# The compression's chunks turned by VectorE in 32x32 blocks instead of by TensorE

## What is computed

```python
def compress(rows, pe, w1, w2):
    B, Tk = rows.shape[:2]
    n_chunk = Tk // CMP_STRIDE
    r = CMP_BLOCK // CMP_STRIDE
    n_cmp = n_chunk - r + 1
    chunks = rows[:, :n_chunk * CMP_STRIDE].reshape(B, n_chunk, CMP_STRIDE, N_KV_HEADS, HEAD_DIM)
    blocks = jnp.concatenate([chunks[:, j:j + n_cmp] for j in range(r)], axis=2) + pe[:, None, :]
    flat = blocks.transpose(0, 1, 3, 2, 4).reshape(B, n_cmp, N_KV_HEADS, CMP_BLOCK * HEAD_DIM)
    return jax.nn.gelu(flat @ w1) @ w2
```

## Time and profile before

| | |
|---|---|
| time, median of 3 runs | 955.6 us (954.11 to 958.27) |
| profiled execution, first to last instruction (its span) | 949.8 us |
| PE busy | 928.6 us (98% of the span) |
| DVE, ACT, POOL busy | 547.0, 195.0, 61.6 us |
| data moved | 260.57 MB, mean 274 GB/s |

### The profile page before, as it was taken

How to read it: one execution, slowest core, us unless ns; L and a number is a source line. 1 busy time by engine, 2 the same in 40 slices (tenths; PEclk the granted TensorE clock), 3 DMA queues, 4 the chain that set the end, 5 groups by cost and what they waited for, 6 DMA issues and landing times.

```text
span 949.8 us, 11382 instructions
## 1 busy us (share of the span) xinstructions
PE 928.6 (98%) x4433; PEld 469.4 (49%) x4433; DVE 547.0 (58%) x1126; ACT 195.0 (21%) x428; POOL 61.6 (6%) x70
## 2 busy tenths in 40 slices
PE   9999999999999999999999999999999999999997
PEld 5565778876554445634343434334334333334443
DVE  3106442547877311664787787787777575768434
ACT  3111211004746202311111111111111111111401
POOL 3100050000000000010000000000000000000000
PEclk9999999999999999999999999999999999999999
DMA  9690354140004792779999999999999999999211
GB/s 309 203 310 0 102 176 150 53 147 1 1 1 116 234 371 105 294 270 405 419 419 418 419 419 421 419 418 419 420 420 419 419 419 420 419 422 402 99 44 50
DMA packets 74874, 260.57 MB, mean 274 GB/s; under 512 B 12554, under 2 KB 36502, under 8 KB 49956
## 3 DMA queue, kind: packets, MB, share of 16 engines
q1 hardware_dynamic: 69568, 248.51, 67.0%
q0 software_dynamic: 4080, 8.93, 2.8%
q10 hardware_dynamic: 1172, 2.40, 0.6%
HBM read 252.72 MB, written 13.08 MB: 280 GB/s over the span
## 4 chain that ended last, share of the span: by engine, by line
PE 80%; SPq 12%; DMA 4%; DVE 2%; POOL 1%; issue 1%; ACT 0%; DVEq 0%
PE ps L1127 72%; SPq L378 12%; DMA w<-in_w_exp_down 3%; PE ps L1508 2%; PE ps L1778 1%; PE ps L1151 1%; DMA h<-in_x_prompt 1%; DMA mixT<-in_state_conv 1%; PE ps L1813 1%; PE ps L1511 0%; PE ps L1317 0%; PE ps L1248 0%; DVE probs L2344 0%; PE ps L1333 0%; POOL gk L718 0%
## 5 line engine op out<-in xcount | busy, mean ns | idle before, releaser
L1127 PE MATMUL ps<-w,xe 128*64 128x512 f32 x1024 | 229.0, 596 | 9.4 <-DMA w<-in_w_exp_up 8.2
L2718 DVE TENSOR_TENSOR h<-h,ps 128x1024 f32<-128x1024 f32 x120 | 143.2, 1215 | 109.4 <-PE ps L1127 109.3
L1127 PEld LDWEIGHTS ps<-w,xe 128*64 128x64 f32 x1024 | 69.8, 137 | 149.6 <-issue 131.8
L1127 PE MATMUL ps<-w,hT 128*64 128x512 f32 x504 | 115.4, 599 | 0.6 <-DMA w<-in_w_exp_down 0.6
L1127 PE MATMUL ps<-yk,ST 128*128 128x512 f32 (+1 forms) x320 | 105.3, 431 | 0.7 <-DVE yk L2708 0.5
L1127 PE MATMUL ps<-xT,wring 128*128 128x272 f32 x384 | 100.4, 401 | 0.0
L1127 PEld LDWEIGHTS ps<-xT,wring 128*128 128x128 f32 x384 | 68.6, 190 | 24.9 <-issue 12.2
L1127 PE MATMUL ps<-wring,xT 128*32 128x128 f32 (+2 forms) x368 | 77.9, 404 | 0.6 <-DVE xT L2013 0.4
L1127 PEld LDWEIGHTS ps<-yk,ST 128*128 128x128 f32 (+1 forms) x320 | 48.6, 174 | 56.9 <-issue 26.7
L1075 ACT ACTIVATE sg<-ps 64x256 f32<-64x256 f32 x64 | 24.1, 377 | 253.6 <-PE ps L1127 243.0
L758 POOL DMA_INDIRECT xg<-hn_rows,sidx x32 | 32.0, 998 | 645.6 <-PE ps L1778 369.7
(11 more groups left out here) (364 smaller groups left out, 877.8 us busy)
## 6 DMA issues: line engine op xcount, KB each, us to landing
w<-in_w_exp_gate SPq DMA_DIRECT2D x64, 1024.0 KB, 22.4
w<-in_w_exp_up SPq DMA_DIRECT2D x64, 1024.0 KB, 26.3
w<-in_w_exp_down SPq DMA_DIRECT2D x63, 1024.0 KB, 24.3
wring<-in_w_in SPq DMA_DIRECT2D x12, 512.0 KB, 6.5
wpg<-in_w_ple_gate SPq DMA_DIRECT2D x2, 2048.0 KB, 19.3
biaslines<-blrow SPq DMA_DIRECT2D x1, 2560.0 KB, 10.4
h<-in_x_prompt SPq DMA_DIRECT2D x4, 512.0 KB, 9.0
wring<-in_w_in SPq DMA_DIRECT2D x2, 1024.0 KB, 8.1
```

Source lines behind the costliest of these rows:

```text
L1127: return nc.tensor.matmul(out, l, r, start=start, stop=stop, skip_group_check=skip)
L2718: TTn(h[0:r, t, :], h[0:r, t, :], both(b, r), ALU.add).then_inc(S["hadd"], 1)
```

## The change

The chunks are now loaded in quarters. The 16 tokens of a chunk are four quarters of 4 tokens (512 numbers, 2 KB); quarter q of a chunk lies on one of the partitions 32q to 32q + 31. Four gathers of 2 KB rows fill `Xk`, four more `Xv` (one for each 32 chunks), with no re-ordering by GpSimd. The prompt's chunks go to `Xp` by one transfer each for keys and values, and pe to `Xpe` by 8 small transfers. VectorE's transpose turns 32x32 blocks inside each group of 32 partitions, so one instruction on 128 partitions x 256 numbers makes 32 columns of all 8 slices of one head at once. For each i there are 10 such instructions and two small copies of pe's columns; one instruction before turns pe itself. The rows of the first matrix are loaded in the order that matches (`first_weights`, 8 KB runs instead of 1 KB). All 48 transposes of `chunk_T` are gone.

```diff
             def back(which):
                 sp.wait_ge(S[f"{which}cmp_out"], 16)
-                r0 = (XC - NCH) * (which == "v")
-                for hh in range(NKV):
-                    sp.dma_start(X2[r0:r0 + SEQ // STRIDE, D * hh:D * (hh + 1)].rearrange("c (r d) -> c r d", d=HD),
-                                 o[f"{which}_cmp_p"].rearrange("(c r) (g d) -> c r g d", r=STRIDE, g=NKV)[:, :, hh, :])\
-                        .then_inc(S["X_in"], 16)
+                x = o[f"{which}_cmp_p"]
+                sp.dma_start(Xp[:, int(which == "v"), :], bass.AP(tensor=x.tensor, offset=x.offset,
+                                                                  ap=[[512, 4], [2048, SEQ // STRIDE], [1, 512]])).then_inc(S["X_in"], 16)
+
+            def first_weights(which):
+
+                sp.dma_start(w1s[:].rearrange("p (h k) n -> p h (k n)", h=2),
+                             a[f"cmp_w1_{which}"].rearrange("(h p k) n -> p h (k n)", h=2, k=8)).then_inc(S["w1_in"], 16)
...
             pool.wait_ge(S["pg_ok"], 1)
-            chunk_rows("k")
-            pool.wait_ge(S["X_pm"], 1)
-            chunk_rows("v")
-            pool.wait_ge(S["X_ev"], 16)
+            for which, to in (("k", Xk), ("v", Xv)):
+                for cb in range(4):
+                    pool.indirect_dma_start(out=to[:, cb, :], out_offset=None,
+                                            in_=a[f"cache_{which}_cmp"].rearrange("g (c r) n -> (g c) (r n)", r=4),
+                                            in_offset=bass.IndirectOffsetOnAxis(ap=pgi[:, NB + cb:NB + cb + 1], axis=0))\
+                        .then_inc(S[f"X{which}_in"], 16)
+            pool.wait_ge(S["X_ev"], 2)
...
                 pe.wait_ge(S["w1_in"], 16 * (i + 1))
-                pe.wait_ge(S["X_ev"], 8 * i + 8)
+                pe.wait_ge(S["X_ev"], i + 1)
...
-            def chunk_columns(i, pp):
-                dve.wait_ge(S["X_tr"], 8 * i + pp + 1)
-                if i and pp == 0:
+            def chunk_columns(i):
+
+
+                dve.wait_ge(S[f"X{'kv'[i]}_in"], 64)
+                if i:
                     dve.wait_ge(S["hid_done"], 2)
-                to = XT[:, pp, :].rearrange("p (g n) -> p g n", g=NKV)
-                if i:
-                    if pp == 0:
-                        V.tensor_copy(XT[:].rearrange("p k (g n) -> p k g n", g=NKV)[:, :, :, NCH:XC], XV[:])
-                    V.tensor_copy(to[:, :, 0:NCH], ps[:, 2 + pp % 2, 0:2 * NCH].rearrange("p (g n) -> p g n", g=NKV)).then_inc(S["X_ev"], 1)
-                else:
-                    x = ps[:, pp % 4, :].rearrange("p (g n) -> p g n", g=NKV)
-                    V.tensor_copy(XV[:, pp, :, :], x[:, :, XC:2 * XC - NCH])
-                    V.tensor_copy(to, x[:, :, 0:XC]).then_inc(S["X_ev"], 1)
-
+                def blocks_of(x, g):
+                    return x.rearrange("p (r g d k) -> p g k r d", r=4, g=NKV, k=8)[:, g, :, :, :]
+
+                for g in range(NKV):
+                    c0 = g * XC
+                    for cb in range(4):
+                        V.transpose(XT[:, :, c0 + 32 * cb:c0 + 32 * cb + 32].rearrange("p k (r d) -> p k r d", r=4),
+                                    blocks_of((Xk, Xv)[i][:, cb, :], g))
+                    V.transpose(XT[:, :, c0 + NCH:c0 + NCH + 32].rearrange("p k (r d) -> p k r d", r=4), blocks_of(Xp[:, i, :], g))
+                    last = V.tensor_copy(XT[:, :, c0 + NCH + 32:c0 + XC], peT[:, i, :, 0:2])
+                last.then_inc(S["X_ev"], 1)
+
+            def chunk_pe():
+
+                dve.wait_ge(S["X_in"], 16 * 10)
+                chain(V.transpose(peT[:], Xpe[:].rearrange("p i (n k) -> p i k n", k=8)))
...
+            chunk_pe()
+            chunk_columns(0)
             for t in range(TT):
                 head_norms(t)
-                for pp in range(3 * t, min(3 * t + 3, 8)):
-                    chunk_columns(0, pp)
                 if t < TP:
                     window_columns(t)
             hidden_bias(0)
             window_columns(TP)
-            for pp in range(8):
-                chunk_columns(1, pp)
+            chunk_columns(1)
```

More of the change, by code:

```diff
@@ L74, in constants @@
     c[:, C_PI] = i % (P // 2)
-    c[:, C_PI + 1] = i % (PAGE // STRIDE)
+    c[:, C_PI + 1] = 4 * (i % (PAGE // STRIDE)) + i // 32
+    c[:, C_JH:C_END] = (i % 32)[:, None] // 8 == np.arange(4)
     head = (i % 32) // NT
@@ L112 @@
 SEMS = """
-M_in X_ev X_in X_pm X_raw X_tr a_exp a_p a_s a_soft asn_ok b_ca b_cd b_pv b_tr bl_out bl_ps bl_sb
+M_in X_ev X_in Xk_in Xv_in a_exp a_p a_s a_soft asn_ok b_ca b_cd b_pv b_tr bl_out bl_ps bl_sb
 bpg_in cb_done cb_ok cm_exp cm_p cm_sub comb cs_out cs_outd cs_ps cst_in ct_done ct_ok cv_done cv_ok
@@ L169, in build @@
         RB = 147.5 * K
-        X1 = at("X1", [P, 2048], RB)
-        X2 = at("X2", [P, 2048], RB + 8 * K)
+        Xk = at("Xk", [P, 4, 512], RB)
+        Xp = at("Xp", [P, 2, 512], RB + 8 * K)
+        Xpe = at("Xpe", [P, 2, 256], RB + 12 * K)
+        peT = at("peT", [P, 2, 8, 32], RB + 14 * K)
         w1s = at("w1s", [P, 16, CH], RB + 16 * K)
@@ L317, in build @@
         jtab = small("jtab", [P, JOBS], I32)
-        pti = small("pti", [P, NPG + 1], I32)
-        pgi = small("pgi", [P, NPG + 1], I32)
+        pti = small("pti", [P, NPG], I32)
+        pgi = small("pgi", [P, NPG + 4], I32)
         sidx = small("sidx", [P, JOBS], I32)
@@ L553, in _ @@
             sp.wait_ge(S["hid_done"], 2)
-            sp.dma_start(w1s[:], a["cmp_w1_v"].rearrange("(k p) n -> p k n", p=P)).then_inc(S["w1_in"], 16)
+            first_weights("v")
             sp.wait_ge(S["tm_norm"], TT)
@@ L1225, in _ @@
                 token_block(2, t)
-            def chunk_bank(i, pp):
-                return 2 + pp % 2 if i else pp % 4
-            def chunk_T(i, pp):
-                if pp == 0:
-                    pe.wait_ge(S["X_pm"], i + 1)
-                if i == pp == 0:
-                    pe.wait_ge(S["X_in"], 16 * 8)
-                if i == pp == 0:
-                    pe.wait_ge(S["bl_sb"], 1)
-                    pe.wait_ge(S["cv_vecc"], 1)
-                held = 2 if i else 4
-                if pp >= held:
-                    pe.wait_ge(S["X_ev"], 8 * i + pp - held + 1)
-                b = chunk_bank(i, pp)
-                for hh in range(NKV):
-                    cols = slice(D * hh + P * pp, D * hh + P * (pp + 1))
-                    c0 = hh * P * (2 - i)
-                    last = T(ps[:, b, c0:c0 + NCH], X1[:, cols], eye(P))
-                    if i == 0:
-                        last = T(ps[:, b, c0 + NCH:c0 + NCH + P], X2[:, cols], eye(P))
-                last.then_inc(S["X_tr"], 1)
             def compress_hidden(i, m):
@@ L1375, in _ @@
             token_block(0, 0)
-            for pp in range(3):
-                chunk_T(0, pp)
-            token_block(0, 1)
-            heads_T(0)
-            for pp in range(3, 6):
-                chunk_T(0, pp)
-            token_block(0, 2)
-            heads_T(1)
-            for pp in range(6, 8):
-                chunk_T(0, pp)
-            token_block(0, 3)
-            heads_T(2)
-            token_block(0, 4)
+            for t in range(1, TT):
+                token_block(0, t)
+                if t < TP:
+                    heads_T(t - 1)
             compress_hidden(0, 1)
```

54 lines of the change are left out of this document (21 added, 33 removed).

## The result

The changed kernel takes 962.3 us (median of 6 runs, 961.94 to 964.96), the kernel before beside it 956.3 us (6 runs, 954.02 to 958.29): a ratio of 1.0059, 95% interval [1.0039, 1.0078]. It is slower, by 0.6%, and outside the range. The profiled execution has a span of 960.1 us and a time of 961.9 us, so 1.8 us lie around the span, not 5.8.

What follows compares the result with a forecast made beforehand. PE was taken as the bound, later the experts' DMA stream that starts on PE's count. Taking 5.3 us off 949.8 gave a 944.5 us span; 955.6 less 5.3 gave 950.3 us, range 948.4 to 953.8.

Steps and rivals of the forecast that it cites:

- What is removed: On PE's path: 48 transposes at about 0.11 us each, 5.3 us less, the values' products starting at 120.5 us.
- Block transposes: On VectorE: 0.42 us each, about 5.2 us ahead of `head_norms(0)` and 4.5 us for values, all hidden, cost nothing.
- The read-back: The prompt's chunks, needed before VectorE's first block: landing at 54 to 58 us, at the latest 59.9, cost nothing.
- the 64 that I had named as a sign of being wrong: On VectorE: a wait on `X_in`, the chunks' arrival, ending past 64 us would show the forecast wrong.
- The rest: Eight gathers for two on GpSimd, about 8 us between 38 and 50 us, and small VectorE operations: all hidden.
- the median of the runs stands 5.8 us above the span: Whole kernel: the 5.8 us between span and median were kept, so a 944.5 us span meant 950.3 us.
- The experts' stream moves along: Experts' stage: the weight stream starts on PE's count, first weights near 411.2 us, so the early gain lasts to the end.
- Dear transposes: Rival, on VectorE: transposes of 0.82 us or more make PE wait; at 1.92 us the time is 973.7 us; chance 0.09.
- late read-back: Rival, ahead of `head_norms(0)`: block ends 4.3 us late, 2.7 us lost after reserve, 953.0 us; chance 0.07.
- no gain: Rival: the experts' stream or a stage between fixes the end, 955.6 us; chance 0.08.

Runs made afterwards that it cites:

- a_again: The changed kernel, unaltered, timed again on a chip where the kernel before takes 950.81 us: 946.83 us, ratio 0.9950.
- a_plain_x: Changed kernel with the chunks' eight gathers replaced by eight ordinary SyncE transfers from the first 16 pages: 959.28 us, ratio 1.0027 to the kernel before.
- a_no_gathers: Changed kernel with all 24 gathers replaced by ordinary SyncE transfers from the first 16 pages: 951.31 us, ratio 1.000 to the kernel before.
- b_again: The kernel before, unchanged, run again to see span and clock of its executions: 956.98 us.
- a_late_x: Changed kernel with the chunks' eight gathers started only near 48 us, after the second column group's first tile is copied: 957.27 us, ratio 1.0008 to the kernel before.
- a_again3: The changed kernel, unaltered, once more, on a chip where the kernel before takes 950.93 us: 947.25 us, ratio 0.9961.
- b_single2: The kernel before with its 16 cache gathers one at a time, each waiting for the last to land: 950.41 us, ratio 0.9998 to the kernel before.
- a_again2: The changed kernel, unaltered, on a chip where the kernel before takes 951.14 us: 948.16 us, ratio 0.9963.

## Why the prediction was wrong

By its own steps, with what was measured:

- **What is removed: 5.3 us.** Right. `a_again` starts the values' products at 120.02 us; the forecast was 120.48, on the scale of an execution whose small sample products start at 42.48 us instead of 42.00. Corrected for the start it is met to 0.02 us. The 390 ns for a transpose by TensorE of the Trainium skill's "VectorE: DVE Perf Modes", section "The three transpose paths", would have made 18.7 us of it; the runs bear out the step of 0.11.
- **Block transposes: 0.42 us each, block 5.2 us.** Too cheap by a quarter to a half: 0.53 from start to start and 0.61 alone, the block 6.6 us, the values' 5.5 instead of 4.5. Within the bounds and hidden. From 256 to 512 elements per partition a transpose grew by 0.49 us (1.10 - 0.61), the elementwise operation of the earlier trace rows by 0.27 us (0.69 - 0.42), so each further element cost 1.8 times as much; the elementwise row was not the right stand-in. The Trainium skill's "Vector Engine (DVE) Microarchitecture Reference", section "3.8 The reshape front-end and per-opcode configuration", has the transposing mode sustain one element per cycle per lane. No row counts cycles, but measured it was slower per element than the elementwise rows, which the prediction had taken for that rate. It read with a stride of 8 elements; no run has another stride.
- **The read-back: 54 to 58 us, at the latest 59.9.** Late. In `a_again` it was issued from 50.27 us and landed at 61.77, 1.9 us past the latest that I had allowed. Its last transfer took 8.0 us from the end of its issue (53.74 us), within the 10.4 assumed; what was late was the issue, behind three loads whose own issue took 4.80 us where it was 2.41. The block ended at 68.4 and ScalarE released `head_norms(0)` after 0.26 us of idling (DVE's row of `a_again` below). So it cost nothing, with no reserve in front of ScalarE left, and in `a_plain_x` and `a_no_gathers`, where eight more transfers stand ahead of it, it cost 1.3 and 1.8 us. In the changed kernel's first profile it landed at 66.13 us, past the 64 that I had named as a sign of being wrong, because SyncE's transfers, too, were released later: `out_k_cmp_p` was issued at 51.09 us, in `a_again` at 43.27.

```profile
61.77 1.11 DVE L2046 STREAM_TRANSPOSE peT<-Xpe 128x512 f32<-128x512 f32 x1 [16.86 <-DMA Xp<-out_v_cmp_p]
...
68.64 0.69 DVE L2005 TENSOR_TENSOR sq<-qn 128x512 f32<-128x512 f32 x1 [0.26 <-ACT qn L809]
```

- **"The rest. Eight gathers in place of two [...] in front of nothing that anyone awaits soon. [...] All hidden."** This is the step that failed. I asked who waits for the gathers and not what runs beside them. In the first comparison PE lost 4.7 us at 42 to 48 us, in the later half of their series, where the two gathers of before cost nothing, and 11.0 us in the second series, where the kernel before in `b_again` lost 4.6 in the same products (148.23 - 126.13 = 22.1 us against 17.5) and 1.4 at the lower clock behind them. Against such an execution of the kernel before the sum is -5.3 + 4.7 + (11.0 - 6.0) = 4.4 us; the two spans differ by 4.1, the medians of the comparison by 6.1, of which the rest is not placed. The first loss is the added gathers', shown on P by `a_late_x` and `a_plain_x`. Why the second is larger is not shown: the series begins 2.9 us ahead of the values' products, where in `b_again` it was 0.6, but in `a_late_x`, with 2.9 us as well, 8.8 were lost. The length of a slow stretch also differs from one execution to the next.
- **"the median of the runs stands 5.8 us above the span", taken to stay.** Wrong, and it should have warned me. Every run whose span is known has 1.8 to 2.0 us around it, and 949.8 + 1.9 = 951.7 us lies below all three runs shown. The profile from which I argued was not an execution of the kind that was timed. That the other 4 us were a slow stretch in the timed ones is inferred from `b_again`, which has one and takes 957 us; whether the profile came from another chip or only from a luckier execution is not known.
- **The experts' stream moves along.** Right but for about 0.5 us. The fourth expert's first weights were issued at 411.75 us in `a_again` (forecast 411.2), with 8 waits and 8.0 us. Ahead of it, PE of `a_again3` waits for the first expert's gathered rows, where `b_single2` on the same chip waited less:

```profile
406.29 0.75 PE L1737 MATMUL ps<-cst,xg 128*128 128x128 f32 x4 [1.15 <-DMA xg<-hn_rows,sidx]
407.89 7.09 PE L1121 MATMUL ps<-w,xe 128*64 128x512 f32 x32 [0.85 <-DVE xe L2640]
```

```profile
410.97 0.75 PE L1779 MATMUL ps<-cst,xg 128*128 128x128 f32 x4 [0.26 <-DMA xg<-hn_rows,sidx]
412.92 2.37 PE L1128 MATMUL ps<-w,xe 128*64 128x512 f32 x10 [1.21 <-DVE xe L2673]
```

- **The rivals.** Dear transposes, late read-back and "no gain" did not decide; the result is slower than no change by a mechanism that I had not named, and 7 in 100 for slower was too little.

On chips without the slow stretches the mechanism and the gain in span would have stood: on R 944.0 and 944.8 us for the changed kernel, where the clock did not dip, against 949.5 for `b_single2` beside them, and 944.5 forecast. The forecast time would not: 946.8 to 948.2 us lie below the range that began at 948.4, because the 5.8 us around the span were 1.9. The medians there differ by 3.0 to 4.0 us, somewhat less than 5.3; 0.5 of the difference is the wait above, and on S, where the medians differ least, the changed kernel's executions had a mean clock of 0.997 against 0.999. The rest I can't place.

**What stays open.** Why PE's instructions come slowly late in a series of gathers, why one series does it and another not, and why on P and not on Q, R and S. Whether it is the gathers as such or something that they share with other traffic was tested only by `a_plain_x`, in the first place. Whether spacing the gathers would cure it was not seen, since no spaced variant came to run on such a chip; moving the first series behind the sample products (`a_late_x`) did cure that place, and brought the changed kernel to even with the one before on P. No version was found that beats the changed kernel on R and S.

## What to carry to other kernels

Before a prediction, hold the profiled execution against the timed ones: if the span plus what commonly lies around it (here 1.9 us) does not give the median, the profile lacks something that the timing has, and a term is missing. A row "issue" on the engine that bounds the kernel is time like any other: look at what the other engines issue in those microseconds, gathers above all, before costing more of them at nothing. And where a small gain decides, time the pair on more than one chip.

## What was unexpected of the hardware

On P, and in the first comparison, whose chip is not known, PE issued an instruction only every 0.70 us, or a multiple of it, for 6 to 9 us in the later part of a series of gathers by GpSimd, while it waited for no semaphore; on Q, R and S never, in twelve profiles, of which only three (`a_again`, `a_again2`, `a_again3`) have the sixteen gathers as dense. Signals from PE were late as well: VectorE's first operation on the sample products started at 43.86 us in `a_again` and at 50.15 in the changed kernel's first profile, more than 4 us after the products that it needs:

```profile
50.15 0.17 DVE L1991 COPY cwT<-ps 128x12 f32<-128x12 f32 x1 [11.29 <-remote]
```

"Remote" is what the trace gives as the releaser there, where that of `a_again` is PE's product. From the later part of the slow stretches on, 3.4 to 10.2 us stood at 1.2 GHz: in the changed kernel 11 instructions of the values' products ran in the 5.6 us from 144.4 us, where in `a_again` 64 took 17.65 us at the full clock, half the time for each.
